# Conv strips in another engine order, their shifted pieces issued by GpSimd, and sixteen more joined units in a two-block network

## The chip, the cores and the metric

The kernel runs on one core of a Trainium2 chip. Its engines have a queue each and run in order: TensorE (PE), VectorE (DVE), ScalarE (ACT), GpSimd (POOL) and SyncE (SP), which issues DMA transfers. They wait for one another by semaphores. The metric is the device time in microseconds, the median of three runs.

## The reference

Two network blocks one after the other, both with two layers, 256 tokens by 1024 features, float32. What matters here, cut from the first block:

```python
mod = cond @ ada_w[i] + ada_b[i]            # cond = silu(c): one row of 1024
h = rms_norm(x, mix_norm_g[i]) * (1.0 + sc1) + sh1
# layer 0: conformer_conv
a, g = jnp.split(h @ w_in + b_in, 2, axis=-1)
u = a * jax.nn.sigmoid(g)
u = lax.conv_general_dilated(u, dw[:, None, :], window_strides=(1,),
    padding=((CONV_WIDTH - 1, 0),), feature_group_count=d) + dw_b   # CONV_WIDTH = 31
u = jax.nn.silu(layer_norm(u, ln_g, ln_b))
y = u @ w_out + b_out
# layer 1: moba_attention, 16 heads with a linear bias, causal softmax, then @ w_o
x = x + g1 * y
h = rms_norm(x, mlp_norm_g[i]) * (1.0 + sc2) + sh2
x = x + g2 * (jnp.square(jax.nn.relu(h @ mlp_w1[i])) @ mlp_w2[i])
```

The second block has a gated mixer (`mixer_a`), a windowed attention with a context (`mixer_b`) and an output projection of each.

## The kernel before

All products run as **units**, 138 of them, listed in `UNITS`. A unit is one weight block of 1 MB (1024 x 256 float32) times the 256 tokens. In the conv stage the units are `conv_a` and `conv_g` in turn (0 to 7, so strip j of the convolution comes from units 2j and 2j+1), then `conv_out` (8 to 11); from 12 (`MLP0`) on the first MLP, from 44 (`QKV`) the attention's inputs, from 56 (`WO`) its output, from 60 (`MLP1`) the second MLP, from 92 and 124 the mixers, from 134 (`B_OUT`) the output.

Weights are streamed. `STREAM` lists 202 pieces of 1 MB: the weight of each unit, and chunks of the modulation matrices `ada_w`, whose places the table `MOD_BEFORE` gives (its list names, for each chunk, the unit ahead of which it stands). `WHERE[s]` is the piece of unit s. SP issues them in order into a ring `raw` of four slots (line 582), and waits before each until DVE has used up the slot's last content. A weight is cut in two: ACT writes its rounded high part (`split_hi`, `w_hi`, line 629), DVE the rest (`split_lo`, `w_lo`, line 1046). A chunk instead goes through `dots` on DVE (line 1079, two halves). PE then does for each of 16 tiles either `three` (lines 1831 to 1833: hi x hi, hi x lo, lo x hi, 256 columns each) or, if the unit is in `JOINED`, `joined` (lines 1837 and 1838: one matmul of 512 columns over the high and low half at once, one of 256). A joined unit leaves two partial sums, so that ACT copies one half (`copy_block`, line 697) and DVE adds the other (`join`, line 1303) before the usual `drain`.

**The conv stage.** The 1024 channels are four **strips** of 256. For strip j ACT takes the sigmoid of g (line 732) and DVE multiplies it with a (`drain` of a `conv_g` unit, line 1319). The result `U` must then be there in 16 shifted copies, each 32 partitions by 568: ten are made by ACT (`shift_copies`, line 675), six by DMA (`BY_DMA`, 71 KB each, line 590). Two sets of buffers serve four strips, so strip 2 waits for the convolution of strip 0, and strip 3 for that of strip 1. DVE also builds blocks of diagonal weights for each strip (`build_blocks`, line 1259). PE convolves a strip in 128 narrow matmuls (line 1816); ACT copies the result out (`conv_copy`, line 682), and PE sums it over the channels (line 1746) for the norm that follows. When all four are done, DVE goes on with the norm (first instruction at line 1600), and only then can unit 8 start.

**What sets the order.** Nothing is planned by the compiler: each engine has a loop `for s in range(FIRST_UNITS, NW + 2)`, and what it does in step s is written out in it by conditions on s. In step s the splits of unit s and the drain of unit s - 2 stand. SP issues the six pieces of strip j behind stream piece `SHIFT_AT[j]`:

```python
for n in range(FIRST_UNITS, NS):
    ...
    sp.dma_start(raw[:, n % RING, :], stream[n])
    for j in range(4):
        if SHIFT_AT[j] == n:
            sp.wait_ge(drained["dve"], DRAINED[2 * j + 1][1])
            ...
```

**Attention 1** is a loop over pairs of heads. In a step DVE takes the biased scores' extrema (`S1`, tiles C and HT, line 1538) and splits an output tile (`XL`, line 1527), ACT takes the exponents (line 836) and copies a turned probability tile for PE (`PT1`, line 842).

## Time and profile before

| | |
|---|---|
| median of three runs | 1223.61 us (1222.88 to 1223.83) |
| the profiled execution | 1222.33 us, of which the span is 1220.5 |
| mean granted TensorE clock | 0.985 |
| busy in the span: PE, DVE, ACT, POOL | 1187.3, 901.1, 585.1, 50.5 us |
| stream pieces | 202 of 1024 KB |

The median stands for the kernel, the profiled execution is the one that all rows come from. PE's busy share is near the whole span, so the chain that ended last is mostly PE; what matters is where it leaves PE.

### The profile page before, as it was taken

How to read it: one execution, taken by the hardware profiler on the slowest of the kernel's cores; microseconds unless marked ns; L12 is line 12 of the kernel's file. 1: busy time of each engine (PE TensorE's matmuls, PEld its weight loads, DVE VectorE, ACT ScalarE, POOL GpSimd, SP SyncE). 2: the span in 40 equal slices, each digit the busy share in tenths (PEclk: the TensorE clock that was granted, in tenths of full speed). 3: DMA queues.
4: the chain of work that ended last, by engine and by line, in shares of the span. 5: the costliest groups of instructions: out<-in, count | busy, mean ns of one | idle time of the engine just before them, and what ended most of it. 6: DMA issues, size and time to landing. Idle time of an engine off the chain costs nothing.

```text
span 1220.5 us, 18749 instructions
## 1 busy us (share of the span) xinstructions
PE 1187.3 (97%) x7746; PEld 1031.3 (84%) x7746; DVE 901.1 (74%) x1355; ACT 585.1 (48%) x776; POOL 50.5 (4%) x69
## 2 busy tenths in 40 slices
PE   8898999999999989999999999999999999999897
PEld 6885988888988869899999888888888888998677
DVE  6778788888878675898877675776757675677666
ACT  4655757556544374764355422332212323454763
POOL 0000000000000040000000000000000000000640
PEclk9998999999989999999999999999999999999998
DMA  9798458877758614667665354333343242342000
GB/s 370 283 289 307 148 218 305 299 289 283 294 191 325 230 52 173 220 245 259 242 250 192 146 196 149 135 109 136 138 172 138 104 144 101 127 139 104 1 2 35
DMA packets 35879, 230.09 MB, mean 189 GB/s; under 512 B 4161, under 2 KB 6465, under 8 KB 9554
## 3 DMA queue, kind: packets, MB, share of 16 engines
q1 hardware_dynamic: 35794, 228.89, 51.5%
q8 instruction: 61, 1.00, 0.3%
q14 instruction: 24, 0.20, 0.0%
HBM read 226.08 MB, written 1.05 MB: 186 GB/s over the span
## 4 chain that ended last, share of the span: by engine, by line
PE 82%; DVE 6%; ACT 5%; DMA 3%; issue 1%; POOL 1%; SPq 1%; ACTq 0%; DVEq 0%
PE prod L1831 18%; PE prod L1832 17%; PE prod L1833 17%; PE prod L1837 11%; PE prod L1838 6%; DMA raw<-stream 3%; DVE w_lo L1046 2%; ACT w_hi L629 2%; PE prod L1798 1%; PE misc L1993 1%; PE misc L1746 1%; PE misc L2095 1%; POOL cond L1029 1%; PE prod L1848 1%; PE misc L1790 1%
## 5 line engine op out<-in xcount | busy, mean ns | idle before, releaser
L1046 DVE TENSOR_TENSOR w_lo<-raw,w_hi 128x2048 fp32r<-128x2048 f32 x131 | 300.2, 2292 | 218.9 <-ACT w_hi L629 218.8
L629 ACT ACTIVATE w_hi<-raw 128x2048 fp32r<-128x2048 f32 x131 | 250.8, 1915 | 398.7 <-PE prod L1833 276.7
L1831 PE MATMUL prod<-X_both,w_hi 128*128 128x256 f32 (+1 forms) x848 | 273.3, 322 | 4.8 <-DVE w_lo L1046 4.1
L1832 PE MATMUL prod<-X_both,w_hi 128*128 128x256 f32 (+1 forms) x848 | 269.5, 318 | 0.0
L1833 PE MATMUL prod<-X_both,w_lo 128*128 128x256 f32 (+1 forms) x848 | 269.4, 318 | 0.0
L1831 PEld LDWEIGHTS prod<-X_both,w_hi 128*128 128x128 f32 x848 | 162.1, 191 | 19.8 <-DVE w_lo L1046 5.7
L1832 PEld LDWEIGHTS prod<-X_both,w_hi 128*128 128x128 f32 x848 | 162.3, 191 | 10.8 <-issue 0.5
L1833 PEld LDWEIGHTS prod<-X_both,w_lo 128*128 128x128 f32 x848 | 162.2, 191 | 10.6
L1837 PE MATMUL prod<-X_both,w_hi 128*128 128x512 f32 x400 | 143.2, 402 | 0.5 <-DVE w_lo L1046 0.5
L1831 PE MATMUL prod<-F_both,w_hi 128*128 128x256 f32 (+1 forms) x448 | 140.8, 314 | 0.0
L1833 PE MATMUL prod<-F_both,w_lo 128*128 128x256 f32 (+1 forms) x448 | 140.4, 313 | 0.0
L1832 PE MATMUL prod<-F_both,w_hi 128*128 128x256 f32 (+1 forms) x448 | 140.4, 313 | 0.0
L1838 PE MATMUL prod<-X_both,w_lo 128*128 128x256 f32 x400 | 112.3, 281 | 0.0
L1079 DVE CUSTOM_DVE_ANT_0 raw<-raw,cond 128x1024 f32<-128x1024 f32 x80 | 94.2, 1218 | 1.2 <-DMA raw<-stream 1.2
L1837 PEld LDWEIGHTS prod<-X_both,w_hi 128*128 128x128 f32 x400 | 75.5, 189 | 20.3 <-DVE w_lo L1046 0.8
L1831 PEld LDWEIGHTS prod<-F_both,w_hi 128*128 128x128 f32 x448 | 85.4, 191 | 5.1
L1833 PEld LDWEIGHTS prod<-F_both,w_lo 128*128 128x128 f32 x448 | 85.4, 191 | 5.0
L1832 PEld LDWEIGHTS prod<-F_both,w_hi 128*128 128x128 f32 x448 | 85.4, 191 | 4.9
L1838 PEld LDWEIGHTS prod<-X_both,w_lo 128*128 128x128 f32 x400 | 75.8, 189 | 0.1
L1837 PE MATMUL prod<-F_both,w_hi 128*128 128x512 f32 x192 | 68.0, 399 | 0.0
L1831 PE MATMUL prod<-w_hi,X_both 128*128 128x256 f32 (+1 forms) x192 | 66.0, 344 | 0.0
L1833 PE MATMUL prod<-w_hi,X_both 128*128 128x256 f32 (+1 forms) x192 | 64.5, 336 | 0.0
(330 smaller groups left out, 1929.1 us busy)
## 6 DMA issues: line engine op xcount, KB each, us to landing
raw<-stream SPq DMA_DIRECT2D x202, 1024.0 KB, 4.9
V<-first_chunks SPq DMA_DIRECT2D x8, 512.0 KB, 12.6
X<-x_features SPq DMA_DIRECT2D x1, 1024.0 KB, 5.7
raw<-first_chunks SPq DMA_DIRECT2D x2, 512.0 KB, 7.0
C<-first_chunks SPq DMA_DIRECT2D x2, 512.0 KB, 17.6
V<-cond_rows SPq DMA_DIRECT2D x1, 1024.0 KB
C<-ctx_features SPq DMA_DIRECT2D x1, 1024.0 KB, 6.9
out_features<-HT SPq DMA_DIRECT2D x4, 256.0 KB, 2.2
```

Of the source, the lines that this page charges most:

```text
L629: A(halves(w)[0], raw[:, n % RING, :].rearrange("p (k c) -> p k c", k=KT), ACT.Copy).then_inc(weight_hi, 1)
L1029: scale(m, m, sm[:, p % 3, 5:6], None, ALU.mult).then_inc(scaled_pool, 1)
L1046: ins = tt(lo, raw[:, n % RING, :].rearrange("p (k c) -> p k c", k=KT), hi.bitcast(F32), ALU.subtract)
L1079: ins = vec.tensor_tensor_reduce(w, w, cond[:, 0, :], 1.0, 0.0, ALU.mult, ALU.add, got[:, 0, k:k + 1])
L1746: ins = mm(misc[:, bank, c:c + T], ones, src[:, k, :], start=(k == 0), stop=(k == count - 1), skip_group_check=True)
L1790: ins = mm(misc[:, b, 0:1], H[:, k, P * b:P * (b + 1)], ones[:, 0:1], start=(k == 0), stop=(k == KT - 1), skip_group_check=True)
L1798: mm(tiles(w, T)[:, 0, :], ones, con[:, 0:T], start=True, stop=True)
L1831: mm(out, lhs_hi, rhs_hi, start=start, stop=False)
L1832: mm(out, lhs_hi, rhs_lo, start=False, stop=False)
L1833: return mm(out, lhs_lo, rhs_hi, start=False, stop=stop)
L1837: mm(out.rearrange("p (h t) -> p h t", h=2), lhs_hi, rhs, start=start, stop=stop)
L1838: return mm(out[:, 0:T], lhs_lo, rhs[:, 0, :], start=False, stop=stop, skip_group_check=True)
```

## The change

Six edits, all of them in what stands where; the arithmetic is the same.

- One modulation chunk stands before unit 6 instead of before unit 9, so units 6, 7 and 8 have their weights one piece later in the stream.
- The six shifted pieces of each strip are issued by POOL, with the same waits, at the start of its program. SP only streams.
- ACT and DVE have another order in the conv stage.
- `JOINED` gets sixteen more units: 56, 57; 67, 68, 70, 72, 73, 75, 77, 78, 80, 82, 83; 134, 135, 136.
- The additions to x (`ON_X`) of units `wo` and `b_out` take part in the rule that `w2` had for the buffer EV.
- In attention 1 ACT's copy of PT1 stands between the two pairs of exponents, and DVE's first pair of maxima ahead of the XL split.

```diff
 for s in (
-    6, 7, 7, 8, 8, 8, 8, 9, 9, 9, 9, 10,
+    6, 6, 7, 7, 8, 8, 8, 8, 9, 9, 9, 10,
...
-SHIFT_AT = [WHERE[6], WHERE[7], WHERE[8] - 1, WHERE[9]]
...
-JOINED = list(range(MLP0, MLP0 + 28)) + [QKV, QKV + 1, QKV + 2, QKV + 4, QKV + 5, QKV + 6] + list(range(MLP1, MLP1 + 6))
+JOINED = list(range(MLP0, MLP0 + 28)) + [QKV, QKV + 1, QKV + 2, QKV + 4, QKV + 5, QKV + 6]
+JOINED += [WO, WO + 1] + list(range(MLP1, MLP1 + 6))
+JOINED += [w for w in range(MLP1 + 6, MLP1 + 24) if MOD_BEFORE[w + 2] == 0]
+JOINED += [B_OUT, B_OUT + 1, B_OUT + 2]
+ON_X = ("w2", "wo", "b_out")
...
-                for j in range(4):
-                    if SHIFT_AT[j] == n:
-                        sp.wait_ge(drained["dve"], DRAINED[2 * j + 1][1])
-                        if j >= 2:
-                            sp.wait_ge(conv_summed, j - 1)
-                        for a, g in BY_DMA:
-                            to, of = shifted(j, a, g)
-                            sp.dma_start(to, of).then_inc(u_shifted[j % 2], 16)
...
+                    def exponents(off):
...
                     if p < KT:
-                        b = p % 3
-                        for off in range(2):
-                            for t, (a, c) in enumerate(((0, P), (P, 3 * P))):
...
+                        exponents(0)
                     if 2 <= p < KT + 2:
                         h = p - 2
                         act.wait_ge(alibi_turned, 2 * h + 1)
                         A(PT1[0][:, h % 2, :], prod[:, 1, 0:3 * P], ACT.Copy).then_inc(alibi_copied_act, 1)
+                    if p < KT:
+                        exponents(1)
...
                 if s == CONV_OUT + 1:
+                    split_hi(CONV_OUT)
+                    conv_copy(1)
                     shift_copies(3)
-                    conv_copy(1)
-                if FIRST_UNITS < s < NW and s not in AHEAD and s not in BEHIND:
+                if FIRST_UNITS < s < NW and s not in AHEAD and s not in BEHIND and s != CONV_OUT:
                     split_hi(s)
...
-                if s in (4, 5, 7):
-                    shift_copies((s - 3) // 2)
+                if s == 5:
+                    shift_copies(0)
                 if s == 7:
+                    shift_copies(1)
                     conv_copy(0)
+                    shift_copies(2)
...
+            for j in range(4):
+                pool.wait_ge(drained["dve"], DRAINED[2 * j + 1][1])
+                if j >= 2:
+                    pool.wait_ge(conv_summed, j - 1)
+                for a, g in BY_DMA:
+                    to, of = shifted(j, a, g)
+                    nc.gpsimd.dma_start(to, of).then_inc(u_shifted[j % 2], 16)
...
+                if s == CONV_OUT + 1:
+                    build_blocks(3)
+                    split_lo(CONV_OUT)
...
-                if s in (3, 4, 6, 8):
+                if s in (3, 4, 7):
                     build_blocks((s - 2) // 2)
```

On ScalarE, from the split of unit 4 on (`w_hi` is a weight's high part, EV the sigmoid of a gate, V and GX from V the shift copies of strip 0), before:

```order
L629 ACTIVATE w_hi<-raw 128x2048
L675 ACTIVATE V<-V 32x568
L675 ACTIVATE GX<-V 32x568
L675 ACTIVATE V<-V 32x568 x3
L675 ACTIVATE GX<-V 32x568
L675 ACTIVATE V<-V 32x568 x3
L675 ACTIVATE GX<-V 32x568
L732 ACTIVATE EV<-prod,col 128x256 x2
L629 ACTIVATE w_hi<-raw 128x2048
```

and with the change:

```order
L624 ACTIVATE w_hi<-raw 128x2048
L727 ACTIVATE EV<-prod,col 128x256 x2
L624 ACTIVATE w_hi<-raw 128x2048
L670 ACTIVATE V<-V 32x568
L670 ACTIVATE GX<-V 32x568
L670 ACTIVATE V<-V 32x568 x3
L670 ACTIVATE GX<-V 32x568
L670 ACTIVATE V<-V 32x568 x3
L670 ACTIVATE GX<-V 32x568
L624 ACTIVATE w_hi<-raw 128x2048
```

The sigmoids of strip 1 and the split of unit 5 have moved ahead of the ten shift copies of strip 0, and the split of unit 6 follows them directly.

On VectorE, where unit 8's weight is split (`w_lo`), the blocks of strip 3 are built (C from con) and strip 3 is multiplied (V from prod, col and EV; the ISA rows are halves of chunks), before:

```order
L1079 ISA raw,dot<-raw,cond 128x1024
L1079 ISA dot 128x1
L1046 TENSOR_TENSOR w_lo<-raw,w_hi 128x2048
L1259 TENSOR_TENSOR C<-con,col 128x2048
L1319 SCALAR_TENSOR_TENSOR V<-prod,col,EV 128x256 x2
L1079 ISA raw,dot<-raw,cond 128x1024
L1079 ISA dot 128x1
```

and with the change:

```order
L1089 ISA raw,dot<-raw,cond 128x1024
L1089 ISA dot 128x1
L1157 TENSOR_TENSOR mod<-dot,col 128x8
L1329 SCALAR_TENSOR_TENSOR V<-prod,col,EV 128x256 x2
L1269 TENSOR_TENSOR C<-con,col 128x2048
L1056 TENSOR_TENSOR w_lo<-raw,w_hi 128x2048
L1089 ISA raw,dot<-raw,cond 128x1024
```

Strip 3's product has moved ahead of its blocks and of unit 8's `w_lo`, which was first of the three.

## Rows read from the trace of the kernel before

**Rows 1.** The page, part 1: busy us, share of span, instructions

```profile
PE 1187.3 (97%) x7746; PEld 1031.3 (84%) x7746; DVE 901.1 (74%) x1355; ACT 585.1 (48%) x776; POOL 50.5 (4%) x69
```

**Rows 2.** chain that ended last, 46:118: start, us, what

```profile
48.24 0.68 ACT V L675
...
55.97 1.80 ACT w_hi L629
...
83.68 7.83 DMA raw<-stream
...
98.78 0.68 ACT SM L675
...
108.85 8.98 PE prod L1816 x128
...
117.86 0.49 DVE V L1600
```

**Rows 3.** timeline of PE: start, us, instruction, [idle before, its end]

```profile
60.15 0.38 PE L1831 MATMUL prod<-X_both,w_hi 128*128 128x256 f32 x1 [3.17 <-DVE w_lo L1046]
...
106.56 2.08 PE L1746 MATMUL misc<-V,con 128*128 128x256 f32 x4 [5.02 <-ACT V L682]
```

**Rows 4.** stretches: us, busy (count) by engine, clock, DMA share, GB/s

```profile
60.00:67.60 7.60, 7.45 (x52) 7.32 (x53) 3.37 (x6) 6.49 (x8) 0.00 (x0) 0.78 0.82 276
...
101.00:118.00 17.00, 11.77 (x147) 6.55 (x139) 15.03 (x28) 10.90 (x15) 0.00 (x0) 0.80 0.94 329
...
78.00:92.00 14.00, 14.00 (x178) 11.63 (x181) 10.31 (x19) 4.94 (x9) 0.00 (x0) 1.00 1.01 323
...
92.00:100.00 8.00, 8.00 (x136) 4.70 (x132) 6.53 (x7) 3.37 (x5) 0.00 (x0) 1.00 1.00 406
```

**Rows 5.** groups of ACT, 45:108: busy us, mean ns, idle before and its releaser

```profile
L629 ACT ACTIVATE w_hi<-raw 128x2048 fp32r<-128x2048 f32 x6 | 11.5, 1912 | 13.4 <-DMA raw<-stream 13.4
```

**Rows 6.** groups of DVE, 45:108, the same columns

```profile
L1079 DVE CUSTOM_DVE_ANT_0 raw<-raw,cond 128x1024 f32<-128x1024 f32 x22 | 25.7, 1221 | 1.2 <-DMA raw<-stream 1.2
...
L1046 DVE TENSOR_TENSOR w_lo<-raw,w_hi 128x2048 fp32r<-128x2048 f32 x5 | 11.5, 2292 | 10.0 <-ACT w_hi L629 10.0
...
L1259 DVE TENSOR_TENSOR C<-con,col 128x2048 f32<-128x2048 f32 x2 | 4.6, 2282 | 0.0
```

**Rows 7.** transfers issued in 62:63 and in 41.4:41.6: KB, us to landing

```profile
raw<-stream SPq DMA_DIRECT2D x1, 1024.0 KB, 8.3
...
raw<-stream SPq DMA_DIRECT2D x1, 1024.0 KB, 4.8
```

**Rows 8.** timeline of SP, the first piece of a strip

```profile
62.78 0.60 SPq L590 DMA_DIRECT2D WS<-V  x1
```

**Rows 9.** groups of POOL, whole span

```profile
L1029 POOL TENSOR_SCALAR cond<-cond,sm 128x512 f32<-128x512 f32 x16 | 31.3, 1960 | 54.7 <-DVE sm L1574 54.7
```

**Rows 10.** timeline of PE, 16 matmuls apart: two joined, two of three

```profile
168.18 0.40 PE L1837 MATMUL prod<-X_both,w_hi 128*128 128x512 f32 x1
...
173.84 0.40 PE L1837 MATMUL prod<-X_both,w_hi 128*128 128x512 f32 x1
...
599.48 0.28 PE L1831 MATMUL prod<-F_both,w_hi 128*128 128x256 f32 x1
...
605.24 0.28 PE L1831 MATMUL prod<-X_both,w_hi 128*128 128x256 f32 x1
```

**Rows 11.** groups of the whole span: a joined unit's copy and addition

```profile
L697 ACT ACTIVATE EV<-prod 128x512 f32<-128x512 f32 x34 | 19.7, 578 | 0.1
...
L1303 DVE TENSOR_TENSOR EV<-prod,EV 128x512 f32<-128x512 f32 x34 | 23.3, 684 | 0.0
```

**Rows 12.** timeline of DVE in attention 1, one turn of the loop apart

```profile
446.67 0.28 DVE L1538 CUSTOM_DVE_ANT_0 C<-prod,SM 128x128 f32<-128x128 f32 x1
...
449.88 0.28 DVE L1538 CUSTOM_DVE_ANT_0 C<-prod,SM 128x128 f32<-128x128 f32 x1
```

**Rows 13.** waits, 430:458: us in total, times, longest

```profile
PE prod L2036 <- ACT C L842: 4.3, 5, 1.5
```

More of the change, by code:

```diff
@@ L694, in copy_block @@
                     act.wait_ge(f_lo, f_index(w - 2) + 1)
-                elif UNITS[w - 2][0] == "w2" and u[0] in ("w1", "w2"):
+                elif UNITS[w - 2][0] in ON_X and u[0] in ("w1", *ON_X):
                     act.wait_ge(x_updated, X_DONE[w - 2])
@@ L752, in drain @@
                     ei = e.rearrange("p (i t) -> p i t", i=2)
-                    if w not in JOINED and w - 2 in JOINED and UNITS[w - 2][0] == "w2":
+                    if w not in JOINED and w - 2 in JOINED and UNITS[w - 2][0] in ON_X:
                         act.wait_ge(x_updated, X_DONE[w - 2])
@@ L829, in attention_1 @@
                         A(XH[:, k, 0:T], misc[:, k % 2, 0:T], ACT.Copy).then_inc(acts_hi, 1)
[L830 to L838 removed]
+                    def exponents(off):
+                        b = p % 3
+                        for t, (a, c) in enumerate(((0, P), (P, 3 * P))):
+                            i = 2 * off + t
+                            act.wait_ge(alibi_max, 4 * p + i + 1)
+                            A(S1[off][:, b, a:c], S1[off][:, b, a:c], ACT.Exp,
+                              bias=sm[:, b, i:i + 1], scale=-1.0,
+                              accum_out=sm[:, b, 4 + i:5 + i]).then_inc(alibi_exp, 1)
+                    if p < KT:
+                        exponents(0)
                     if 2 <= p < KT + 2:
@@ L954, in _ @@
                     copy_block(s - 2)
-                if s - 3 in JOINED and UNITS[s - 3][0] != "w2":
+                if s - 3 in JOINED and UNITS[s - 3][0] not in ("w2", "b_out"):
                     drain(s - 3)
@@ L1523, in attention_1, with maxima @@
                 for p in range(a, b):
+                    def maxima(off):
+                        b = p % 3
+                        slope = 2.0 ** (-8.0 * (2 * p + off + 1) / HEADS)
+                        for t, (a, c) in enumerate(((0, P), (P, 3 * P))):
+                            i = 2 * off + t
+                            vec.tensor_tensor_reduce(
+                                S1[off][:, b, a:c], score_pair(p)[:, 512 * off + a:512 * off + c],
+                                alibi[:, a:c], -slope, 3.0e38, ALU.add, ALU.min,
+                                sm[:, b, i:i + 1]).then_inc(alibi_max, 1)
+                    if p < KT:
+                        dve.wait_ge(alibi_scored, p + 1)
+                        if p >= 3:
+                            dve.wait_ge(alibi_turned, 2 * (p - 3) + 2)
+                        maxima(0)
                     if p >= 5 and p < KT + 5:
@@ L1529, in attention_1 @@
                     if p < KT:
-                        b = p % 3
-                        dve.wait_ge(alibi_scored, p + 1)
-                        if p >= 3:
-                            dve.wait_ge(alibi_turned, 2 * (p - 3) + 2)
-                        for off in range(2):
-                            slope = 2.0 ** (-8.0 * (2 * p + off + 1) / HEADS)
-                            for t, (a, c) in enumerate(((0, P), (P, 3 * P))):
-                                i = 2 * off + t
-                                vec.tensor_tensor_reduce(
-                                    S1[off][:, b, a:c], score_pair(p)[:, 512 * off + a:512 * off + c],
-                                    alibi[:, a:c], -slope, 3.0e38, ALU.add, ALU.min,
-                                    sm[:, b, i:i + 1]).then_inc(alibi_max, 1)
+                        maxima(1)
                     if 1 <= p <= KT:
@@ L1679, in _ @@
                         dots(BESIDE[s], (0,))
-                    if s > FIRST_UNITS and s not in AHEAD and s not in BEHIND and s != CONV_OUT + 1:
+                    if s > FIRST_UNITS and s not in AHEAD and s not in BEHIND and s not in (CONV_OUT, CONV_OUT + 1):
                         split_lo(s)
```

5 lines of the change are left out of this document (removed).

## The prediction

> **What bounds the kernel now.** I read the busy shares first. TensorE works 97% of the span [rows 1], so only three things can bring much: its idle time, its time at the low clock, and less time per streamed column. Then the chain that ended last, in order of time. In the conv stage, 46 to 118 us, it leaves TensorE: it runs over ScalarE's shift copies (0.68 us each, ten a strip), the split of a weight, a wait of 7.83 us for a transfer, ScalarE's copies again, the last strip's convolution (8.98 us) and DVE's first instruction on that at 117.86 [rows 2]. TensorE's own timeline has the two gaps that this costs: 3.17 us ahead of unit 5, whose w_lo came late, and 5.02 us ahead of the sums over strip 1, which waited for ScalarE's copy of it [rows 3]. Around each gap the granted clock is low, 0.78 of full speed over 7.6 us and 0.80 over 17 us, against 1.00 between [rows 4].
>
> Why ScalarE is late: strip 0's ten copies, from 48.24 on, 6.9 us in all, and the two sigmoids stand before unit 5's w_hi, which so starts at 55.97 [rows 2]. Of its idle time 13.4 us is a wait for the weight stream [rows 5]; DVE waits 10.0 us for w_hi [rows 6]. The stream is late because the DMA engines are full: share 1.01 at 323 GB/s from 78 to 92 us, where strip 2's pieces run, and 1.00 at 406 GB/s from 92 to 100 [rows 4]. A 1 MB chunk so costs 1.05/406 = 2.6 us of all 16 engines, and six pieces (0.44 MB), by what is missing at 323, (406 - 323)/406 x 14 + 0.44/406 = 3.9 us. A chunk issued at 62.4 into that queue landed after 8.3 us, one issued at 41.5 after 4.8 [rows 7].
>
> **The change part by part.**
>
> *ScalarE's order.* The sigmoids of strip 1 and w_hi(5) now stand ahead of strip 0's copies. Unit 4 ends at 60.15 - 3.17 = 56.98 [rows 3], unit 3 one unit of 5.8 us earlier [rows 10], 51.2. So: sigmoids (0.85) to 52.0, w_hi(5) to 53.9 (1912 ns [rows 5]), w_lo(5) to 56.2 (2292 ns [rows 6]). The gap of 3.17 us is gone, and with it the low clock: (1 - 0.78) x 7.6 = 1.7. Strip 0's copies end at 60.8, and unit 5, which covers them, at 62.8: 2.0 us of cover; every us beyond that would stop conv 0.
>
> *What is late next.* TensorE after unit 5: conv 0 (8.98 x 0.80 = 7.1 at full clock) to 69.9, unit 6 to 75.7. Unit 7's weight is now stream piece 11, not 10, as one chunk stands earlier. Piece 10 landed at 70.7 [rows 7]; one chunk more is 2.6, of which the stream, no longer stopped on SP, wins back some 0.7: 72.6. Then w_hi(7) to 74.5 and w_lo(7) to 76.8: unit 7 is 1.1 late and ends at 82.6. ScalarE: strip 1's copies to 81.4, copy of bank 0 to 82.3, strip 2's copies to 89.2, sigmoids to 90.1, w_hi(8) to 92.0, copy of bank 1 to 92.9, strip 3's copies to 99.8. Before, strip 3's copies began at 98.78, behind a w_hi(8) whose piece came at 91.5 (83.68 + 7.83) [rows 2]. TensorE: conv 1 to 89.7, sums of strip 0 to 90.8, conv 2 to 97.9, sums of strip 1 to 99.0, then conv 3 from 99.8 instead of 108.85 [rows 2], done at 107.
>
> *DVE* has the same instructions in another order. Four chunks (12 to 15) to 89.3, product of strip 3 to 90.9, blocks 3 (2282 ns [rows 6]) to 93.1, w_lo(8) to 95.4, three chunks to 102.3. Blocks 3 have 6.7 us of cover before conv 3 needs them; without it each us would be a late conv 3.
>
> *The end of the stage* is then the stream again. Piece 20, unit 9's weight, needs the slot of piece 16, free with w_lo(8) at 95.4, and lands 8.3 us later, at 103.7 [rows 7]. w_hi(9) to 105.7, w_lo(9) to 108.0, and behind it DVE adds squares and takes earlier tiles, about one instruction of 2.3 us in sum (an estimate; from nothing to 4), so the step of 117.86 comes at 110.3. **Gain 7.5 us.** Were the stream never late, it would be the gaps and the clock, 3.17 + 5.02 + 1.7 + 0.20 x (2.08 + 8.98) = 12.1 [rows 2 to 4], less about 1 for DVE behind the last strip: 11, the upper end. The lower: with 4.5 us of DMA time a strip and 2.7 a chunk the pieces up to 20 land about 4 later, which leaves 3.
>
> *The 24 pieces on POOL.* SP loses 24 issues of 0.60 us [rows 8], 3.6 us of a stopped stream per strip; the bytes stay, so the DMA engines' 3.9 us a strip stay. POOL is idle here. What an issue costs on it no row shows. From below it is SP's 0.60 [rows 8], from above POOL's longest instruction, 1960 ns [rows 9]. An issue computes nothing, so it is nearer to the first: I take 1.0. Strip 3's pieces are released by its product at 90.9 and needed at 99.8; they are there at 90.9 + 6p + 3 for the landing, at p = 1.0 at 99.9: no loss. At p = 1.96 conv 3 starts at 105.7 and ends at 112.8: a gain of 5 instead of 7.5 (3 if the clock falls in the gap).
>
> The Trainium skill speaks against this part: "DMA: Bandwidth & Descriptors", section Issuing engines are not separate DMA queues, says that transfers of all issuers run on the same 16 DMA engines, and that another issuer saves only the usually small time on the sequencer. The trace agrees on the first half, with the share of 1.01 in [rows 4]; by the second half the sum would take little from this part, and the conv gain would be the reordering's alone.
>
> *JOINED.* Sixteen more units (2 of wo, 11 of the last MLP, 3 of the output) go from 48 matmuls of 256 columns to 16 of 512 and 16 of 256, the same column count in fewer instructions. A joined unit takes 173.84 - 168.18 = 5.66 us, one of three 605.24 - 599.48 = 5.76 [rows 10]: 16 x 0.10 = 1.6 us. Each adds 0.578 us on ScalarE and 0.684 on DVE [rows 11]. In the MLP the splits are 1.9 + 2.3 = 4.2 of a unit's 5.7 us, so the additions are hidden, except where a chunk's dots (2 x 1.2 [rows 6]) fall in the same step on DVE: 2.3 + 2.4 + 0.7 + 0.7 = 6.1. The edit picks units with no chunk two units on, so I price it at nothing; without that cover it costs 0.4 x 11 = 4.4. At the output units the last join stands before the closing sums: 0.2 lost. **Gain 1.4.**
>
> *Attention 1.* ScalarE copies PT1 between the two pairs of exponents, and DVE takes the first maxima ahead of the XL split. The loop takes 449.88 - 446.67 = 3.21 us [rows 12], and TensorE waited 4.3 us in all for the copy, five times [rows 13]. With XL off that path the loop falls to the sum of DVE's instructions in it, about 2.75: 0.45 over three or four steps. **Gain 1.6**, from 0.5 to 2.5.
>
> **Sum.** 7.5 + 1.4 + 1.6 = 10.5. The profiled execution took 1222.33 us (span 1220.5 and 1.8 around it), 1.3 below the median of 1223.61. So 1211.8 on its scale, and 1213.1 as a median.
>
> **The rivals.**
> 1. *The stream is never late*: conv 11, total 14, 1209.6. For it: SP is freed of 14.4 us of issues. Against: the share of 1.01 [rows 4].
> 2. *Slow pieces*, p = 1.96: conv 5, total 8, 1215.6. As a mechanism here: DVE is busy 10.31 of 14 and 6.53 of 8 us [rows 4], with instructions of 2.29 us; if POOL can't write a piece's descriptors while one of them runs, each piece waits up to that long. The Trainium skill, "SBUF — State Buffer", section SBUF: two separate sides, says that a transfer issued by GpSimd starves while DVE runs in a two-port mode; no row here shows such a wait.
> 3. *The transfers get in each other's way*: the pieces, issued earlier, run ahead of weights that are needed sooner. Conv 3, total 6, 1217.6.
> 4. *Slower than before*, by the pieces' price. Conv 3 ends at the low clock at 90.9 + 6p + 3 + 9.0 = 102.9 + 6p; against 117.83 before, and with 3.0 gained elsewhere, it decides from p = 3.0 on. At p = 4 it is 126.9: 1229.6 as a median. For it: nothing but that no row prices the issue. Against: it is above all of POOL's rows [rows 9].
> 5. *Nothing measurable*: the MLP's chunk steps cost their 4.4 beside rival 3: 6 - 4.4, 1222.0.
>
> **Chances.** Forecast (conv 6 to 9) 0.47, rival 1 0.20, rival 2 0.15, rival 3 0.10, rival 4 0.05, rival 5 0.03. A measurement of this kernel can tell 0.2%, 2.4 us, from no change. Faster by more 0.92, within it 0.03, slower 0.05. The range 1208 to 1218.5 runs from below rival 1 to above rival 3 and leaves out rivals 4 and 5 and the far ends of the others.
>
> **What would show it.** Unit 5 without a gap, near 57; w_hi(8) done before 93; conv 3 from near 100 at a clock above 0.95; 24 issues on POOL of about 1 us; the last MLP's joined units 5.66 us apart with no idle; an attention loop below 2.9 us. Wrong would make it: issues over 1.3 us, pieces that land more than 3 us after issue, piece 11 after 73, or w_lo late in the last MLP.

## The result, and the profile after

The changed kernel took 1214.57 us (median of five runs, 1209.66 to 1214.90) against 1222.88 us of the kernel before, measured beside it: ratio 0.9928, 95% interval 0.9914 to 0.9942. The forecast was 1213.1 in 1208 to 1218.5. The profiled execution took 1212.37 us (span 1210.5) where 1211.8 was forecast on the profiled scale; six further runs gave a median of 1212.38 and a ratio of 0.9901 (0.9879 to 0.9923). A gain of 0.7 to 1.0% is small, but both intervals lie clear of 1.

TensorE's line of the page, for [rows 1]:

```profile
PE 1181.1 (98%) x7490; PEld 1014.1 (84%) x7490; DVE 910.5 (75%) x1371; ACT 592.2 (49%) x792; POOL 63.3 (5%) x93
```

Its busy time fell by 6.2 us and the span by 10.0: 3.8 us of idle time went. To see where, I took one event that both kernels have, ScalarE's split of a weight (`w_hi`, which starts in the steady stages when TensorE ends a unit), and compared its start at the ends of the stages:

| | before, us | after, us | after minus before |
|---|---|---|---|
| first split behind the conv stage | 131.97 | 125.11 | -6.86 |
| ahead of attention 1 | 424.22 | 417.49 | -6.73 |
| in the tail of attention 1 | 463.59 | 455.41 | -8.18 |
| last ahead of wo's norm | 475.11 | 466.83 | -8.28 |
| start of the second MLP | 494.74 | 485.69 | -9.05 |
| second MLP, four units in | 517.97 | 508.92 | -9.05 |
| behind its last joined unit, 83 | 634.29 | 624.09 | -10.20 |
| last split of the program | 1195.01 | 1184.56 | -10.45 |
| end of the span | 1220.5 | 1210.5 | -10.0 |

So the conv stage gave 6.9 us, attention 1.5, the way over wo's norm 0.8, the MLP 1.15, and the output units gained 0.25 and lost 0.45 behind it.

These are differences of one trace each. For the conv stage there is a measure of the scatter: the repetition of the changed kernel and three of the experiments below (each half of attention 1, and `JOINED` as before) leave that stage as it is. In the five traces it ended at 125.11, 126.32, 128.16, 124.33 and 125.62 us, a gain of 3.8 to 7.6 with a median of 6.4. Counted from the split of unit 4, the second split of all, it took 78.1 to 80.8 us, against 85.67 before. The kernel before has one trace only. A difference of 1 or 2 us in where this stage ends therefore says nothing of an edit by itself.

**The conv stage.** TensorE's timeline, for [rows 3]: the gap of 3.17 us ahead of unit 5 and that of 5.02 ahead of the sums are gone, and three smaller waits stand in their place.

```profile
77.56 0.39 PE L1849 MATMUL prod<-X_both,w_hi 128*128 128x256 f32 x1 [1.52 <-DVE w_lo L1056]
...
101.06 0.38 PE L1834 MATMUL prod<-WS,C 128*32 128x256 f32 x1 [1.28 <-DMA BS<-V]
...
110.65 0.49 PE L1772 MATMUL misc<-con,HT 128*128 128x1 f32 x3 [2.48 <-DVE HT L1213]
```

Unit 7's weight was late, conv 3 waited for a shifted piece (BS from V, a DMA) and started at 101.06, where 108.85 stood before, and the third wait is that of the norm for DVE's work on strip 3. The chain that ended last, for [rows 2], says why:

```profile
62.88 10.07 DMA raw<-stream
...
72.97 1.92 ACT w_hi L624
...
105.69 2.20 DVE w_lo L1056
```

It runs over the landing of piece 11 (until 72.95), unit 7's split, ScalarE's two strips of copies, the sigmoids, DVE's products and unit 9's w_lo: the stream again, as in the forecast. DVE's instruction on the last strip, at 117.86 in [rows 2], is now at 110.51, and ScalarE's splits of units 8 and 9 start at 90.30 and 103.22, the second behind a wait of 3.41 us for its piece:

```profile
110.51 0.48 DVE L1615 SCALAR_TENSOR_TENSOR V<-prod,col,rows 128x256 f32<-128x256 f32 x1
...
90.30 1.91 ACT L624 ACTIVATE w_hi<-raw 128x2048 fp32r<-128x2048 f32 x1
...
103.22 1.91 ACT L624 ACTIVATE w_hi<-raw 128x2048 fp32r<-128x2048 f32 x1 [3.41 <-DMA raw<-stream]
```

The stretches, for [rows 4]. The columns are us, busy time (count) of PE, PEld, DVE, ACT and POOL, clock, DMA share and GB/s. The first stretch is now at the full clock, and a low one has come between 112 and 118. The last line is the kernel before, right behind its gap of 5.02 us, at half speed:

```profile
60.00:67.60 7.60, 7.60 (x114) 5.66 (x116) 2.73 (x5) 3.39 (x5) 0.00 (x0) 1.00 1.02 327
...
78.00:92.00 14.00, 14.00 (x187) 10.39 (x189) 12.87 (x21) 13.76 (x21) 0.15 (x1) 1.00 1.02 386
...
92.00:100.00 8.00, 7.78 (x132) 4.45 (x120) 8.00 (x9) 7.68 (x13) 3.01 (x6) 1.00 1.02 310
...
106.00:112.00 6.00, 3.52 (x53) 2.58 (x43) 5.41 (x9) 2.94 (x6) 0.00 (x0) 1.00 0.96 360
...
112.00:118.00 6.00, 6.00 (x28) 5.32 (x27) 4.71 (x13) 2.99 (x6) 0.00 (x0) 0.72 0.02 10
...
106.00:112.00 6.00, 5.22 (x36) 2.95 (x40) 5.20 (x11) 5.33 (x7) 0.00 (x0) 0.50 1.04 343
```

The DMA engines are as full as before (1.02 at 386 GB/s where 323 stood: strip 2's pieces now run earlier).

**POOL.** The 24 issues took about 0.53 us each, which [rows 8, 9] could only bound:

```profile
91.85 0.54 POOL L1026 DMA_DIRECT2D WS<-V  x1 [17.69 <-DVE V L1329]
...
94.48 0.53 POOL L1026 DMA_DIRECT2D BS<-V  x1
```

The last piece of strip 3 was issued by 95.0, and conv 3 got it at 101.06: not 1.0 us an issue and 3 to land, but 0.53 and 6. The landing time could have been read from the kernel before. Here are the pieces of strips 0 and 2, median us from issue to landing, of the kernel before (SP) and the changed one (POOL):

```profile
V<-V SPq DMA_DIRECT2D x10, 71.0 KB, 7.5
...
V<-V POOLq DMA_DIRECT2D x10, 71.0 KB, 7.5
```

**Attention 1 and the rest.** One turn of the loop, for [rows 12], is 441.80 - 438.89 = 2.91 us instead of 3.21:

```profile
438.89 0.29 DVE L1540 CUSTOM_DVE_ANT_0 C<-prod,SM 128x128 f32<-128x128 f32 x1
...
441.80 0.29 DVE L1540 CUSTOM_DVE_ANT_0 C<-prod,SM 128x128 f32<-128x128 f32 x1
```

From 520 us to the end of the second MLP's joined units TensorE has one wait, 0.25 us for w_lo, behind a stretch (600 to 612) in which DVE was busy 11.18 of 12 us; and in the last unit of the output the copy and the join stand on the chain ahead of the closing sums, where before the last product did:

```profile
617.98 0.38 PE L1849 MATMUL prod<-F_both,w_hi 128*128 128x256 f32 x1 [0.25 <-DVE w_lo L1056]
...
1190.16 0.61 ACT EV L692
...
1190.79 0.70 DVE EV L1313
```

### The profile page after: what moved, and what is told of

The parts are those of the page before. It is cut to its first block, busy times and chain, and to the rows that moved or that the text cites. A ratio compares the mean times of both kernels' runs of the same rounds, so it can differ in the third digit from the quotient of the medians.

```text
span 1210.5 us, 18282 instructions
## 1 busy us (share of the span) xinstructions
PE 1181.1 (98%) x7490; PEld 1014.1 (84%) x7490; DVE 910.5 (75%) x1371; ACT 592.2 (49%) x792; POOL 63.3 (5%) x93
## 3 DMA queue, kind: packets, MB, share of 16 engines
HBM read 226.08 MB, written 1.05 MB: 188 GB/s over the span
## 4 chain that ended last, share of the span: by engine, by line
PE 81%; DVE 7%; ACT 4%; DMA 4%; issue 2%; POOL 1%; SPq 1%; ACTq 0%; DVEq 0%
PE prod L1855 16%; PE prod L1849 15%; PE prod L1851 15%; PE prod L1850 15%; PE prod L1856 8%; DMA raw<-stream 2%; DVE w_lo L1056 2%; DMA WS<-first_chunks 2%; PE prod L1816 1%; PE misc L2011 1%; ACT w_hi L624 1%; PE misc L2113 1%; POOL cond L1039 1%; PE misc L1764 1%; PE misc L1808 1%
## 5 line engine op out<-in xcount | busy, mean ns | idle before, releaser
L1849 PE MATMUL prod<-X_both,w_hi 128*128 128x256 f32 (+1 forms) x656 | 218.0, 332 | 2.6 <-DVE w_lo L1056 2.2
L1850 PE MATMUL prod<-X_both,w_hi 128*128 128x256 f32 (+1 forms) x656 | 214.5, 327 | 0.0
L1851 PE MATMUL prod<-X_both,w_lo 128*128 128x256 f32 (+1 forms) x656 | 214.4, 327 | 0.0
L1855 PE MATMUL prod<-X_both,w_hi 128*128 128x512 f32 x592 | 211.5, 401 | 1.9 <-DVE X_both L1289 1.2
L1856 PE MATMUL prod<-X_both,w_lo 128*128 128x256 f32 x592 | 166.1, 281 | 0.0
L1849 PEld LDWEIGHTS prod<-X_both,w_hi 128*128 128x128 f32 x656 | 124.5, 190 | 16.6 <-DVE w_lo L1056 4.3
L1855 PEld LDWEIGHTS prod<-X_both,w_hi 128*128 128x128 f32 x592 | 111.3, 188 | 31.6 <-DVE X_both L1289 2.0
L1850 PEld LDWEIGHTS prod<-X_both,w_hi 128*128 128x128 f32 x656 | 124.5, 190 | 11.0 <-issue 0.5
L1849 PE MATMUL prod<-F_both,w_hi 128*128 128x256 f32 (+1 forms) x384 | 122.8, 320 | 0.2 <-DVE w_lo L1056 0.2
L1850 PE MATMUL prod<-F_both,w_hi 128*128 128x256 f32 (+1 forms) x384 | 122.3, 318 | 0.0
L1855 PE MATMUL prod<-F_both,w_hi 128*128 128x512 f32 x256 | 90.5, 398 | 0.0
L1849 PEld LDWEIGHTS prod<-F_both,w_hi 128*128 128x128 f32 x384 | 72.9, 190 | 6.1 <-DVE w_lo L1056 0.9
L1850 PEld LDWEIGHTS prod<-F_both,w_hi 128*128 128x128 f32 x384 | 72.9, 190 | 5.0
L1856 PE MATMUL prod<-F_both,w_lo 128*128 128x256 f32 x256 | 71.9, 281 | 0.0
L1849 PE MATMUL prod<-w_hi,X_both 128*128 128x256 f32 (+1 forms) x192 | 66.0, 344 | 0.0
```

The costliest lines, as they stand in the source:

```text
L1849: mm(out, lhs_hi, rhs_hi, start=start, stop=False)
L1850: mm(out, lhs_hi, rhs_lo, start=False, stop=False)
L1851: return mm(out, lhs_lo, rhs_hi, start=False, stop=stop)
L1855: mm(out.rearrange("p (h t) -> p h t", h=2), lhs_hi, rhs, start=start, stop=stop)
L1856: return mm(out[:, 0:T], lhs_lo, rhs[:, 0, :], start=False, stop=stop, skip_group_check=True)
```

## The experiments

Times are medians; a ratio is to the kernel before, measured beside it, with its 95% interval. That kernel had 1223.64 us beside the first four experiments, 1223.95 beside DVE's half of attention 1, the halved pieces, the repetition and the last version, and 1222.39 beside the rest. Since single runs of one kernel spread over 2 to 8 us (what is known of the reason is in the last section), most readings come from the traces: the start of the first split behind the conv stage (131.97 before; 125.11 in the changed kernel, 124.33 to 128.16 over the five traces with its conv stage) and the intervals between such splits.

**The pieces on SP again.** ScalarE's and DVE's new order stays.

```diff
+SHIFT_AT = [WHERE[6], WHERE[7], WHERE[8] - 1, WHERE[9]]
+                for j in range(4):
+                    if SHIFT_AT[j] == n:
+                        sp.wait_ge(drained["dve"], DRAINED[2 * j + 1][1])
...
-            for j in range(4):
-                pool.wait_ge(drained["dve"], DRAINED[2 * j + 1][1])
```

> The changed kernel with only the six pieces of each strip issued by SP again, at SHIFT_AT of before. Theory (SP's stops cost stream time, and strip 3's pieces, behind piece 20, come late): conv stage 3 us longer than with POOL, about 1217.5 us, SP issues 0.6 us each. Rival (the order alone brought the gain, the issuer is indifferent since all transfers share the 16 DMA engines): 1214.5, within 0.5 of the changed kernel, first weight split after the stage within 0.5 us of its place.

Measured: 1216.32 us, 0.9936 (0.9913 to 0.9958); the stage ended at 129.13, 4.0 us later than with POOL and 2.8 earlier than before. TensorE's and SP's timelines:

```profile
105.97 0.61 PE L1836 MATMUL prod<-WS,C 128*32 128x256 f32 x1 [7.91 <-DMA BS<-V]
...
95.07 0.60 SPq L594 DMA_DIRECT2D WS<-V  x1
```

Conv 3 waits 7.91 us for a piece: strip 3's were issued only from 95.07 on, behind stream piece 20, though its product was there at 89.9 (DVE's products began at 88.99), and each took 0.60 us and more. The order alone is worth 2.8 us here; what POOL adds is 4.0 against the changed kernel's first trace and 3.5 against the median of the five. From unit 4's split to its end the stage took 82.92 us, longer than in all five (78.1 to 80.8), so the rival, less than 0.5 us at the stage's end, is wrong; the medians alone, with intervals that overlap, would not say so.

**The pieces on POOL alone**, in the kernel before.

```diff
-                for j in range(4):
-                    if SHIFT_AT[j] == n:
...
+            for j in range(4):
+                pool.wait_ge(drained["dve"], DRAINED[2 * j + 1][1])
```

> The kernel before with only the pieces on POOL. Theory: piece 15 is no longer held 2.7 us behind strip 2's issues, so unit 8's w_hi starts at about 88.5 to 89 instead of 91.5 and the stage ends about 3 us earlier, near 1220. Rival (order alone): no change, 1222.9, w_hi at 91.5. The gap of 3.17 us ahead of unit 5 stays by both.

Measured: 1220.46 us, 0.9971 (0.9955 to 0.9987); stage end 130.39, 1.6 us earlier than before. The gap ahead of unit 5 stays, 3.33 us, and unit 8's split starts at 90.33:

```profile
59.72 0.58 PE L1829 MATMUL prod<-X_both,w_hi 128*128 128x256 f32 x1 [3.33 <-DVE w_lo L1044]
...
90.33 1.91 ACT L620 ACTIVATE w_hi<-raw 128x2048 fp32r<-128x2048 f32 x1 [8.20 <-DMA raw<-stream]
```

The stream was 1.2 us earlier, not 2.5 to 3. The median is 3.2 us below the kernel before. In the trace the gain is 4.1: 1.6 stand at the end of the stage, and the rest comes in the first MLP's units (1.0), at the norm behind it (0.8) and at wo's norm (0.75), where nothing was edited. So 2.8 by the order and 1.6 by the issuer make 4.4 if they were independent; together they gave 3.8 to 7.6 over the five traces, median 6.4. That each opens the way for the other is likely and not shown, with one trace for each part: with the old order ScalarE is late whatever the stream does, with the old issuer strip 3's pieces stand behind the stream.

**The chunk back ahead of unit 9.**

```diff
-    6, 6, 7, 7, 8, 8, 8, 8, 9, 9, 9, 10,
+    6, 7, 7, 8, 8, 8, 8, 9, 9, 9, 9, 10,
```

> The changed kernel with the one modulation chunk back ahead of unit 9. Theory (the stream decides, and piece 20 is unit 9's weight either way): the gap of 1.52 us ahead of unit 7 goes, but the stage ends at the same time within 0.5 us, 1214.5. Rival (the gap ahead of unit 7 is on the path): 1.5 us faster. Second rival (the chunk's move was needed to take load off DVE ahead of unit 9): 1 to 2 us slower.

Measured: 1214.90 us, 0.9930 (0.9903 to 0.9957). Unit 7 had no gap, and conv 3 started at 98.20. The profile puts its wait of 0.51 us down to the issue, but the last piece, issued at 92.06, landed after 6.1 us, at 98.16, and that is what it waited for. But w_lo of unit 9 was where it had been, so DVE's last step came at 110.68 (110.51 in the changed kernel), TensorE idled 5.50 us ahead of the norm instead of 2.48, and the clock was low behind the idle time:

```profile
98.20 0.38 PE L1834 MATMUL prod<-WS,C 128*32 128x256 f32 x1 [0.51 <-issue]
...
110.82 1.44 PE L1772 MATMUL misc<-con,HT 128*128 128x1 f32 x6 [5.50 <-DVE HT L1213]
...
112.00:118.00 6.00, 6.00 (x23) 5.46 (x23) 3.39 (x10) 1.49 (x2) 0.00 (x0) 0.50 0.03 14
```

The stage ended at 127.19, 2.1 us later than in the changed kernel's first trace; 1.9 of it came behind DVE's last step, at this clock. The first part of the theory held (gap gone, last step unchanged), the end did not, and neither rival names the reason. Since the five traces with an unaltered stage reach 128.16, no run shows that the edit costs anything.

**One more chunk later**, ahead of unit 10 instead of 9.

```diff
-    6, 6, 7, 7, 8, 8, 8, 8, 9, 9, 9, 10,
+    6, 6, 7, 7, 8, 8, 8, 8, 9, 9, 10, 10,
```

> The changed kernel with one more chunk moved, from ahead of unit 9 to ahead of unit 10. Theory (piece 20's landing at 103.2 and the w_lo behind it set the end of the stage): unit 9's weight is piece 19, lands 2.6 us earlier, and the step at 110.51 comes 1.5 us earlier, about 1213. Rival (strip 3's pieces and conv 3 set the end): less than 0.4 us.

Measured: 1211.69 us, 0.9907 (0.9879 to 0.9935). Unit 9's w_lo started at 102.76 instead of 105.6, as forecast; now conv 3, which had waited 2.69 us for a piece and ran at the low clock, was last, and DVE's step came at 110.09:

```profile
101.58 0.61 PE L1834 MATMUL prod<-WS,C 128*32 128x256 f32 x1 [2.69 <-DMA BS<-V]
...
102.76 2.29 DVE L1056 TENSOR_TENSOR w_lo<-raw,w_hi 128x2048 fp32r<-128x2048 f32 x1
...
110.09 0.48 DVE L1615 SCALAR_TENSOR_TENSOR V<-prod,col,rows 128x256 f32<-128x256 f32 x1 [1.99 <-PE prod L1834]
```

Both things that the theory and its rival name lie within half a microsecond of each other: taking one away leaves the other. The stage ended at 124.22, but the chunk that now stands ahead of unit 10 made the way from there to the split ahead of the MLP 12.90 us instead of 11.52, so that this split came at 137.12, later than the changed kernel's 136.63.

**Both at once, with unit 83 and 136 out of `JOINED`.**

```diff
-    6, 6, 7, 7, 8, 8, 8, 8, 9, 9, 9, 10,
+    6, 7, 7, 8, 8, 8, 8, 9, 9, 9, 10, 11,
-JOINED += [w for w in range(MLP1 + 6, MLP1 + 24) if MOD_BEFORE[w + 2] == 0]
+JOINED += [w for w in range(MLP1 + 6, MLP1 + 23) if MOD_BEFORE[w + 2] == 0]
-JOINED += [B_OUT, B_OUT + 1, B_OUT + 2]
+JOINED += [B_OUT, B_OUT + 1]
```

> The changed kernel with the chunk back ahead of unit 9, two others moved from ahead of unit 9 and 10 to ahead of 10 and 11 (list 6, 7, 7, 8, 8, 8, 8, 9, 9, 9, 10, 11), and without units 83 and 136 in JOINED. Theory: conv 3 starts at 98.2 as in the run with the chunk back, and w_lo(9) ends 2.6 us earlier as in the run with the chunk later, so PE has no long wait, its clock stays up, and the stage ends 3 to 4 us before the changed kernel's; plus 0.5 at unit 83 and 0.25 at unit 136: 1210. Rival: the chunk ahead of unit 11 makes w_lo(11) or the split ahead of the MLP late and gives the gain back: 1213 to 1214.

Measured: 1211.32 us, 0.9907 (0.9892 to 0.9922). DVE's step on the last strip came at 107.86, 2.7 us earlier than in the changed kernel, but the stage ended at 123.56, only 1.6 earlier where the theory had 3 to 4: TensorE still waited 1.36 us for the last piece and 2.25 ahead of the norm, and from 112 to 118 its clock was 0.62. The split ahead of the MLP was at 136.41 against 136.63, so 1.3 us were given back, as the rival says. Unit 83 made no difference: the last six steps of the MLP's joined part took 34.58 us without and 34.57 with it. Without unit 136 the end of the span lay 25.44 us behind the last split, not 25.94.

**Attention 1, ScalarE's half alone.** DVE's order as before.

```diff
-                    if p < KT:
-                        dve.wait_ge(alibi_scored, p + 1)
-                        ...
-                        maxima(0)
                     if p >= 5 and p < KT + 5:
                         ...
                     if p < KT:
+                        dve.wait_ge(alibi_scored, p + 1)
+                        ...
+                        maxima(0)
                         maxima(1)
```

> The changed kernel with DVE's order in attention 1 as before (XL split ahead of both maxima), only ScalarE's copy between the exponents. Theory (the XL split, which waits for ScalarE's XH copy, is what paced the loop): the loop goes back to about 3.1 to 3.2 us a turn, 1.2 to 1.6 us lost. Rival (PE's wait for the PT1 copy paced it, so ScalarE's half is what counts): loop at 2.8, less than 0.4 us lost.

**DVE's half alone.** ScalarE's order as before.

```diff
                     if p < KT:
                         exponents(0)
+                        exponents(1)
                     if 2 <= p < KT + 2:
                         ...
-                    if p < KT:
-                        exponents(1)
```

> The changed kernel with ScalarE's order in attention 1 as before (copy of PT1 behind all four exponents), only DVE's maxima ahead of the XL split. Theory (the XL split's wait paced the loop, and DVE's half is what counts): a turn in 2.9 us, as in the changed kernel. Rival (both halves are needed: with all exponents first, the copy that PE waits for is late again): 3.0 to 3.2 us a turn, 0.4 to 1.2 us lost.

Measured: 1215.16 us, 0.9942 (0.9923 to 0.9960), and 1213.71, 0.9918 (0.9890 to 0.9946). One turn of the loop with ScalarE's half alone, then with DVE's:

```profile
439.66 0.28 DVE L1540 CUSTOM_DVE_ANT_0 C<-prod,SM 128x128 f32<-128x128 f32 x1
...
442.86 0.28 DVE L1540 CUSTOM_DVE_ANT_0 C<-prod,SM 128x128 f32<-128x128 f32 x1
...
439.95 0.29 DVE L1539 CUSTOM_DVE_ANT_0 C<-prod,SM 128x128 f32<-128x128 f32 x1
...
442.86 0.29 DVE L1539 CUSTOM_DVE_ANT_0 C<-prod,SM 128x128 f32<-128x128 f32 x1
```

That is 3.20 and 2.91 us: ScalarE's half alone gives nothing, DVE's alone gives all of it, in the loop and between the splits around the attention (30.25 us; 30.24 in the changed kernel, 31.25 before; with ScalarE's half alone 32.76, of which some 1.7 is a low clock, 0.64 from 418 to 420 and 0.51 from 420 to 422 us). The XL split's wait for ScalarE was what paced it.

**`JOINED` as before.**

```diff
-JOINED += [WO, WO + 1] + list(range(MLP1, MLP1 + 6))
-JOINED += [w for w in range(MLP1 + 6, MLP1 + 24) if MOD_BEFORE[w + 2] == 0]
-JOINED += [B_OUT, B_OUT + 1, B_OUT + 2]
+JOINED += list(range(MLP1, MLP1 + 6))
```

> The changed kernel with JOINED as before (none of the sixteen added units). Theory (0.10 us each): 1.1 us lost over the second MLP, net of the 0.5 that unit 83 gives back 0.6 to 1.2, 0.2 at wo, and the end of the kernel the same or 0.2 us better: in all 0.7 to 1.7 us slower. Rival (the joins at wo shorten the wait ahead of the MLP, where the changed kernel gained 0.8): 0.8 lost at wo too, in all 2.0 to 2.5.

Measured: 1210.79 us over four runs that spread from 1208.33 to 1214.34, 0.9906 (0.9882 to 0.9931). By its median this is the faster kernel, by its trace it isn't; the runs' spread hides an effect of this size, and the trace is of the slowest of the four. The splits that bound the second MLP, in this kernel and in the changed one:

```profile
510.17 1.92 ACT L622 ACTIVATE w_hi<-raw 128x2048 fp32r<-128x2048 f32 x1 [1.93 <-PE prod L1854]
...
626.39 1.92 ACT L622 ACTIVATE w_hi<-raw 128x2048 fp32r<-128x2048 f32 x1 [2.03 <-PE prod L1849]
...
508.92 1.92 ACT L624 ACTIVATE w_hi<-raw 128x2048 fp32r<-128x2048 f32 x1 [1.94 <-PE prod L1856]
...
624.09 1.92 ACT L624 ACTIVATE w_hi<-raw 128x2048 fp32r<-128x2048 f32 x1 [2.02 <-PE prod L1851]
```

116.22 and 115.17 us: the eleven units are worth 1.05, or 0.095 each. That is net of what the end of the joined units costs: the last of these steps took 6.26 us in the changed kernel and 5.76 here. Over the output units the changed kernel is 0.2 us shorter to the last split (12.62 against 12.83) and 0.5 longer behind it (25.9 against 25.4). Over wo's norm the interval was 19.48 us here, 19.63 before and 18.86 in the changed kernel, but 18.88 in the run with POOL alone, where wo isn't joined either: the 0.8 us there came with the clock (0.89 and 0.83 of full speed from 480 to 492 us before, 1.00 in the changed kernel), and not with the joins.

**SP, with each strip at an earlier place in its queue.**

```diff
-SHIFT_AT = [WHERE[6], WHERE[7], WHERE[8] - 1, WHERE[9]]
+SHIFT_AT = [WHERE[6] - 1, WHERE[6], 12, 19]
```

> The changed kernel with the pieces on SP, but each strip at the earliest place in SP's queue at which SP would wait anyway: behind stream pieces 7, 8, 12 and 19. Theory (what cost time on SP was the place in its queue, strip 3 behind piece 20, not the issuing): conv 3 starts at 101 to 102 and the stage ends within 1 us of the changed kernel. Rival (SP's 3.6 us of issues a strip hold the stream up at any place): stage 2 to 3 us longer, as in the first run with SP.

Measured: 1216.28 us, 0.9949 (0.9931 to 0.9968); stage end 131.71. Part of that is not the edit's: the clock was 0.79 from 30 to 38 us, before any piece, and the second split was already 2.3 us late (49.10 against 46.82). The rest is 4.3 us. Strip 1's issues held SP until 61.15, so that stream piece 9 went out at 61.19 (56.56 in the changed kernel, of which 2.3 is that late start), and unit 7 waited 3.55 us:

```profile
61.19 2.72 SPq L586 DMA_DIRECT2D raw<-stream  x3
...
82.77 0.39 PE L1851 MATMUL prod<-X_both,w_hi 128*128 128x256 f32 x1 [3.55 <-DVE w_lo L1058]
```

The theory is wrong, and the rival holds. From unit 4's split to its end the stage took 82.61 us, as good as the 82.92 with the pieces at their old places in SP's queue: what an earlier place saves for the strip, it costs in the stream.

**Each piece issued as two halves.** The same bytes in 48 issues.

```diff
-                    nc.gpsimd.dma_start(to, of).then_inc(u_shifted[j % 2], 16)
+                    for i in range(2):
+                        nc.gpsimd.dma_start(to[:, i:i + 1, :], of[:, i:i + 1, :])...
```

> The changed kernel with each of the 24 pieces issued as two halves, 48 issues on POOL, the bytes the same. It prices an issue on POOL: at 0.53 us each, strip 3's last is issued 3.2 us later, near 98.2. Theory (the pieces' landing is what conv 3 waits for): conv 3 starts 3 us later, near 104, and the stage ends 2 us later, since w_lo(9) covers the first us. Rival (the pieces wait for their turn in the full DMA engines and not for their issue): conv 3 less than 1 us later.

Measured: 1211.88 us, 0.9897 (0.9874 to 0.9919). The last issue ended at 97.3 instead of 95.0, and conv 3 started at 102.67:

```profile
96.30 0.98 POOL L1027 DMA_DIRECT2D BS<-V  x2
...
102.67 0.38 PE L1835 MATMUL prod<-WS,C 128*32 128x256 f32 x1 [3.36 <-DMA BS<-V]
```

In the five traces of the unaltered stage it started at 100.36 to 103.22 (101.06 and 102.58 in those of the changed kernel itself). So the 3 us of the theory did not come, and what did lies inside that scatter: conv 3 waits mostly for the landing, in DMA engines whose share is 1.00 then. An effect of the issuing of 1 or 2 us this run can't exclude.

**The changed kernel again, unaltered.**

> The changed kernel once more, unaltered, with a trace of its own. Theory (the stretches at the low clock, 3.4 us each, fall or don't fall at the same few places from run to run, and each costs up to 1.7 us): the times of single runs spread again over 4 to 5 us, the places of the weight splits agree within 0.3 us in stretches at full clock, and differ by 1 to 2 us only where one trace has such a stretch. Rival (the first trace is typical to 0.3 us throughout): all splits agree within 0.3 us.

Measured: 1212.38 us (1208.83 to 1215.76), 0.9901 (0.9879 to 0.9923). The stage ended at 126.32 and conv 3 waited 3.26 us for its piece; ahead of attention the split was at 418.00 (417.49 in the first trace), the MLP took 115.28 us (115.17). The rival, agreement to 0.3 us throughout, is wrong; of the theory the spread of the runs held, but the 1.2 us at the end of the conv stage came with a wait and a low clock together:

```profile
102.58 0.60 PE L1834 MATMUL prod<-WS,C 128*32 128x256 f32 x1 [3.26 <-DMA BS<-V]
```

**A version with the other chunk list.** The list of the kernel above, only unit 136 out of `JOINED`.

> The changed kernel with the chunk list 6, 7, 7, 8, 8, 8, 8, 9, 9, 9, 10, 11 and without unit 136 in JOINED (unit 83 stays in). Theory: the stage ends 2.5 us before the changed kernel's in the same call, 1 to 1.5 of that is lost again ahead of the MLP, the end of the kernel takes 25.4 us after the last weight split instead of 25.9: in all 1.5 to 2 us faster. Rival: no difference that can be told from the runs' own spread.

Measured: 1208.77 us (1207.86 to 1214.53), 0.9880 (0.9858 to 0.9903), beside 1212.38 of the changed kernel. Conv 3 started at 98.83, and DVE's step on the last strip came at 108.08. The profile names nothing for TensorE's wait of 1.42 us ahead of conv 3, but the last piece, issued at 91.76, landed 7.0 us later, at 98.76, so conv 3 waited for its piece here too:

```profile
98.83 0.38 PE L1834 MATMUL prod<-WS,C 128*32 128x256 f32 x1 [1.42 <-issue]
...
BS<-V POOLq DMA_DIRECT2D x1, 71.0 KB, 7.0
...
108.08 0.48 DVE L1615 SCALAR_TENSOR_TENSOR V<-prod,col,rows 128x256 f32<-128x256 f32 x1
```

The stage ended at 124.44, 1.9 us before the repetition's (2.5 forecast), of which 1.2 were given back ahead of the MLP; behind the last split it took 25.8 us, not the 25.4 that were forecast without unit 136. These leave 0.7 and 0.2 us. The last split came 4.6 us before the repetition's, and most of that lies where the edit touches nothing: at the norm ahead of the first MLP (18.2 us from unit 12's split to unit 13's, against 20.1) and in that MLP's units (99.9 against 101.8).

It is the fastest of all by its median, 1.2% below the kernel before. That it also beats the changed kernel is likely and not settled: the two intervals overlap (0.9858 to 0.9903, 0.9879 to 0.9923); pooled, the two versions with this list had a median of 1210.2 over ten runs, the changed kernel 1212.8 over eleven.

## Why the prediction was right

Point by point, in its own order:

- *ScalarE's order:* as forecast. Unit 5 without a gap, w_hi(5) at 52.30 (52.0 forecast), the clock from 60 to 67.6 at 1.00.
- *What is late next:* piece 11 landed at 72.95 (72.6), unit 7 was 1.52 us late (1.1), w_hi(8) started at 90.30 (90.1). Conv 3 started at 101.06, not 99.8, because it waited for its piece.
- *DVE:* in the forecast order and times; strip 3's blocks were done at 93.5 (93.1).
- *The end of the stage:* piece 20 landed at 103.2 (103.7), the step of 117.86 came at 110.51 (110.3). At that step the gain was 7.4 us (5.4 to 8.0 over the five traces), at the end of the stage 6.9 (3.8 to 7.6, median 6.4), 7.5 forecast. What the sum left out is the clock behind the step: 0.72 of full speed between 112 and 118. From the step to the end of the stage it took 14.1 us before, 14.6 in the changed kernel, and 14.1 to 16.5 in the other traces. The forecast took the low clock as bound to the two old gaps.
- *The 24 pieces:* the price was off in both halves, 0.53 us for the issue instead of 1.0 and about 6 for the landing instead of 3. That the forecast came within 1.1 us is luck: 90.9 + 6 x 1.0 + 3 = 99.9 against 91.85 + 6 x 0.53 + 6 = 101.0, where two errors nearly cancel. No row stood behind the 3 us, and the trace of the kernel before had the landing of these pieces, 5.2 to 7.5 us by tile. The issue at 0.53 us rules out rivals 2 and 4, which needed 1.96 and 3.0; the run with twice the issues shows that the landing counts for more.
- *The rule on issuers:* that transfers of all issuers run on the same 16 DMA engines, as the Trainium skill's page "DMA: Bandwidth & Descriptors" (section Issuing engines are not separate DMA queues) says, agrees with the traces: with POOL as issuer the share was 1.02 and the pieces landed after 6.0 to 7.9 us (median by tile), in the same kernel with SP after 6.4 to 7.5. The rows of the kernel before, with SP as the only issuer, could not show it. The conclusion against this part of the change was wrong. What counts is less the 0.6 us per issue than what stands behind it in a queue that has to wait: with SP strip 3 stood behind a stream piece, or the stream behind a strip. The two runs with SP show one each.
- *Descriptors held back by DVE:* nothing shows it. POOL's issues took 0.53 to 0.60 us each, also while DVE ran two instructions of 2.28 us back to back from 91.23 to 95.7, and the pieces landed as late when SP issued them (the last one of strip 3 after 6.9 us on SP and 6.5 on POOL). The Trainium skill's page "SBUF — State Buffer" (section SBUF: two separate sides) says that a transfer issued by GpSimd starves while DVE runs in a two-port mode; no row tells whether these instructions run in it, and no run here shows such a wait.
- *JOINED:* 1.15 us in the MLP (1.1 forecast), 0.1 us at wo's units; at the output 0.25 gained and 0.45 lost (0.3 and 0.2 forecast). In all 1.05, not 1.4. The run without the joins confirms the MLP's 0.095 us a unit.
- *Attention 1:* 1.5 us (1.6), the turn 2.91 us, not 2.75. The last three turns were 3.21 us each before and are 2.46, 2.91 and 2.91 now, so the size came from 0.75 + 0.30 + 0.30 and not from 0.45 in each. The half that does it is DVE's, which the forecast named as the path.
- *Its own signs of being wrong:* two of them came. The pieces landed far more than 3 us after issue, and w_lo was late once in the last MLP, by 0.25 us; the turn missed its 2.9 by a hair. The total held all the same, because conv 3 had to wait only 1.3 us for its piece.

The sum, 10.5, stands against 10.0 in the profiled executions and 8.3 (1222.88 less 1214.57) and 11.6 (1223.95 less 1212.38) in the two comparisons of medians. The parts are 6.9 + 1.05 + 1.5 = 9.4 in the first trace, each below its forecast; 0.8 more came at wo's norm by TensorE's clock, which the forecast had counted only in the conv stage. So the mechanism of each part is right, and the nearness of the total owes something to luck: with the median of the five conv stages the parts make 8.9. The mean granted clock went from 0.985 to 0.991, which is (0.991 - 0.985) x 1210 = 7 us at most, less where TensorE waits anyway.

## What to carry to other kernels

Where a queue issues both a stream and small transfers that wait for a result, the price of the small ones isn't only their issue time: it is the wait at the head of the queue, for whatever stands behind. An otherwise idle engine takes that wait without cost; here it was worth some 3.5 us with the new order (2.2 to 4.8 over the traces) and 1.6 in the one trace without, so try such edits together before dropping one.

Before you price a transfer on another issuer, read how long it takes to land on the old one.

Price a join or a copy that a cheaper matmul form needs at the end of the stage too: 0.1 us a unit is gained in the steady stage, and one joined unit ahead of a closing sum costs 0.5 (0.2 by another trace).

When single runs spread by 5 us, read an edit of 1 us from the trace, between two instructions that bound its stage, and repeat the unaltered kernel to see what that interval does by itself: here the length of the conv stage moved by 2.7 us between traces, that of the second MLP by 0.1. And where the profile puts a wait down to nothing, look up when the transfers landed.
